# Mix projection of a two-layer encoder trunk: six of eight output tiles as block products

## What is computed

```python
mix = (jax.nn.sigmoid(gate_a) * y_a + jax.nn.sigmoid(gate_b) * y_b) @ w_out
x = x + rmsnorm(mix, g_post_mix)
```

## Time and profile before

| what | value |
|---|---|
| runs before | 1815.65, 1816.67, 1817.83 us (median 1816.67) |
| the profiled execution | 1816.42 us, its span 1814.6 us |
| PE busy | 1800.7 us, 99% of the span |
| DVE, ACT, POOL busy | 1115.6, 713.4, 1115.1 us |
| chain that ended last | PE 89%, DVE 7%, ACT 1%, issue 1% |
| granted clock of TensorE | 1.0 in the whole span |
| mix projection, layer 0 | 404.4 to 452.56 us, layer 1 the same 900 us later |

### The profile page before, as it was taken

How to read it: one execution, slowest core, us unless ns; L and a number is a source line. 1 busy time by engine, 2 the same in 40 slices (tenths; PEclk the granted TensorE clock), 3 DMA queues, 4 the chain that set the end, 5 groups by cost and what they waited for, 6 DMA issues and landing times.

```text
span 1814.6 us, 34638 instructions
## 1 busy us (share of the span) xinstructions
PE 1800.7 (99%) x14006; PEld 1742.6 (96%) x14006; DVE 1115.6 (61%) x1952; ACT 713.4 (39%) x1485; POOL 1115.1 (61%) x1292
## 2 busy tenths in 40 slices
PE   9999999999999999999999999999999999999999
PEld 8998989999999999999999988899999999999999
DVE  6676775332778568554657767752337795785554
ACT  4444453112556245332334444531135552552321
POOL 8685634656555845957666864346465558459484
...
DMA packets 76239, 170.54 MB, mean 94 GB/s; under 512 B 6384, under 2 KB 34160, under 8 KB 76080
## 3 DMA queue, kind: packets, MB, share of 16 engines
...
## 4 chain that ended last, share of the span: by engine, by line
PE 89%; DVE 7%; ACT 1%; issue 1%; POOL 0%; DMA 0%; SPq 0%; DVEq 0%; ACTq 0%; POOLq 0%
PE ps L1980 61%; PE ps L2418 6%; PE ps L2033 4%; PE ps L2448 3%; PE ps L2161 3%; PE ps L2119 2%; DVE xT L1723 1%; PE ps L2072 1%; DVE mix L1719 1%; DVE R L1364 1%; DVE xn L1364 1%; PE ps L2215 1%; DVE RF L1817 1%; PE ps L2221 1%; PE ps L2020 1%
## 5 line engine op out<-in xcount | busy, mean ns | idle before, releaser
L1980 PE MATMUL ps<-xn,wsp 128*128 128x272 f32 x7728 | 989.8, 289 | 2.1 <-ACT R L1065 0.8
L1980 PEld LDWEIGHTS ps<-xn,wsp 128*128 128x128 f32 x7728 | 974.0, 189 | 6.8 <-issue 3.0
L774 POOL TENSOR_TENSOR wsp<-raw,wsp 128x256 fp32r<-128x256 f32 x448 | 358.2, 821 | 17.9
L769 POOL CAST wsp<-raw 128x512 fp32r<-128x512 f32 x224 | 150.6, 672 | 184.6 <-DMA raw<-in_wstream 129.3
L760 POOL TENSOR_TENSOR wsp<-raw,wsp 128x256 fp32r<-128x256 f32 x208 | 151.3, 761 | 178.7 <-ACT wsp L950 178.7
L787 POOL TENSOR_TENSOR wsp<-raw,wsp 128x256 fp32r<-128x256 f32 (+1 forms) x174 | 213.3, 1248 | 6.6
L1980 PE MATMUL ps<-R,wsp 128*128 128x272 f32 x1632 | 209.1, 289 | 0.1
L1980 PEld LDWEIGHTS ps<-R,wsp 128*128 128x128 f32 x1632 | 206.0, 189 | 1.3 <-DVE xT L1393 0.5
L780 POOL CAST wsp<-raw 128x1024 fp32r<-128x1024 f32 (+2 forms) x102 | 91.3, 906 | 171.6 <-DMA raw<-in_wstream 152.7
L1364 DVE SCALAR_TENSOR_TENSOR R<-ps,R 128x512 fp32r<-128x512 f32 (+13 forms) x272 | 129.5, 499 | 65.3 <-ACT R L869 19.0
L754 POOL TENSOR_TENSOR wsp<-raw,wsp 128x512 fp32r<-128x512 f32 x64 | 94.6, 1498 | 47.3 <-DVE raw L1817 23.8
...
## 6 DMA issues: line engine op xcount, KB each, us to landing
raw<-in_wstream SPq DMA_DIRECT2D x233, 512.0 KB, 3.6
...
raw<-in_kc SPq DMA_DIRECT2D x8, 512.0 KB, 3.5
raw<-in_vc SPq DMA_DIRECT2D x8, 512.0 KB, 4.5
...
```

What stands on the lines that cost most here:

```text
L769: nc.gpsimd.tensor_copy(dst[:, 0, f], part[:, f]).then_inc(S["w_hi"], 1)
L774: ins = nc.gpsimd.tensor_tensor(dst[:, 1, f], part[:, f], dst[:, 0, f].bitcast(F32), ALU.subtract)
L1980: mm = pe.matmul(z[:, h], w[:, x, (k0 + k) * P:(k0 + k + 1) * P], rhs[:, y, k, h * HT:(h + 1) * HT], start=(k == 0 and (x, y) == (0, 0)), ...
```

## The change

`out` 0 and `out` 7 stay plain tiles. The other six become the pairs (1, 4), (2, 5), (3, 6), each made by seven block products. P1 of the first pair is put before the last k-tile of `out` 0. The activation blocks come from new work in `gated_b`: the mix tiles j = 0 to 3 and j = 4 to 7 are the two halves of k; T1, T2, T3 are sums of their column halves. `ga` 7 and `gb` 7 move ahead of `ya` 4, because the second half of the mix and its T3 are put in the place of `xn`, so that `ya` 4 to `yb` 7 follow one another without a gate tile between. ACT takes the highs of 16 more chunks per layer. x comes back in eight DMAs with chunk loads between them. The products of the mix projection use the PSUM banks in an order of their own. The helpers of the block products are now shared by both projections (their bodies are the same but for the lookup of the pair) and not shown.

```diff
+OUT = -1
+BLOCK_PAIRS = {OUT: [(1, 4), (2, 5), (3, 6)], **{i: [(j, j + NP) for j in range(NP)] for i in range(LAST)}}
...
-         ("ga", 6), ("gb", 6), ("ya", 4), ("yb", 4), ("ga", 7), ("gb", 7), ("ya", 5), ("yb", 5), ("ya", 6), ("yb", 6),
+         ("ga", 6), ("gb", 6), ("ga", 7), ("gb", 7), ("ya", 4), ("yb", 4), ("ya", 5), ("yb", 5), ("ya", 6), ("yb", 6),
...
-STREAM += [("out", j) for j in range(KT)] + [("pp", 0)] + FFN
+OUT_ORDER = [0] + [m for pair in BLOCK_PAIRS[OUT] for m in pair] + [KT - 1]
+STREAM += [("out", j) for j in OUT_ORDER] + [("pp", 0)] + FFN
...
-CAST = [c for n, c in enumerate(STREAM) if c[0] in UP and STREAM[n - 6][0] in UP]
+CAST = STREAM[ST_AT[("proj", 2)]:ST_AT[("out", 0)] + 1] + [("out", KT - 1), ("pp", 0), ("upg", 0)]
+CAST += [c for n, c in enumerate(STREAM) if c[0] in UP and STREAM[n - 6][0] in UP]
...
+                ring = [4, 5] + freed[2:] + freed[:1] + [6, 7] + freed[1:2] if t == OUT else freed + [4, 5, 6, 7]
                 continue
...
+                    sp_.wait_ge(S["mi_raw"], M_RAW[KT - 1, "B"])
                     if layer > 0:
                         sp_.wait_ge(pre["x_st"], 16)
-                    sp_.dma_start(xT[:], x_dram if layer > 0 else x_in.rearrange("(k p) t -> p k t", p=P)).then_inc(pre["x_back"], 16)
+                    x_from = x_dram if layer > 0 else x_in.rearrange("(k p) t -> p k t", p=P)
+                    behind = {1: ("out", 3), 2: ("out", 6), 3: ("out", 7), 5: ("pp", 0)}
+                    for k in range(KT):
+                        if k in behind:
+                            load_to(ST_AT[behind[k]])
+                        sp_.dma_start(xT[:, k], x_from[:, k]).then_inc(pre["x_back"], 16)
...
+                    def mix_high(j):
+
+                        kk = j % NP
+                        act.wait_ge(S["mi_raw"], M_RAW[j, "B"])
+                        ac(mix_plain(j, 0), m_raw[:, j // NP, kk], ACT.Copy).then_inc(S["mi_hi"], 1)
+                        n = G_T1 if j < NP else G_T2
+                        act.wait_ge(S["mi_raw"], M_RAW[j, n])
+                        ac(mix_part(kk, 0, n), m_keep[:, kk], ACT.Copy).then_inc(S["mi_hi"], 1)
+                        if j >= NP:
+                            act.wait_ge(S["mi_raw"], M_RAW[j, G_T3])
+                            ac(xn[:, 0, 2 * kk + 1], m_raw[:, 0, kk], ACT.Copy).then_inc(S["mi_hi"], 1)
+
...
                     for n, j in MIXES:
                         if n == "yb":
-                            act.wait_ge(S["mi_raw"], j + 1)
-                            ac(mixin[:, 0, j], tmp[0], ACT.Copy).then_inc(S["mi_hi"], 1)
+                            if j == KT - 1:
+                                plain_high(OUT, 0)
+                                for m in ("S1", "S2", "S3"):
+                                    sum_high(OUT, 0, m)
+                            mix_high(j)
                         elif n in ("ga", "gb"):
                             gate((n, j))
+                        if (n, j) in SPLIT_AFTER:
+                            cast(SPLIT_AFTER[(n, j)])
 
 
                     nc.scalar.preload_act_table_set("natural_log_exp_and_others")
-                    for j in range(KT):
-                        if j < KT - 1:
-                            z = tile(("out", j))
-                            if j == 0:
-                                act.wait_ge(S["dve_read"], dread(("yb", KT - 1)))
-                            square(0, j, z)
+                    hand_on(OUT, 0, "P1", "P2")
+                    sum_high(OUT, 0, "S4")
+                    z = tile(("out", 0))
...
+                        more = j < len(BLOCK_PAIRS[OUT]) - 1
+                        if j > 0:
+                            hand_on(OUT, j, "P1", "P2")
+                        if more:
+                            plain_high(OUT, j + 1, ("A11",))
+                        hand_on(OUT, j, "P6", "P3")
+                        if more:
+                            plain_high(OUT, j + 1, ("A22",))
+                            for m in ("S1", "S2", "S3"):
+                                sum_high(OUT, j + 1, m)
                         else:
-                            z = ptile(("out", j))
-                            for h, part in enumerate((("half", 0), ("out", j))):
-                                act.wait_ge(S["p_done"], AT[part] + 1)
-                                square_half(0, h, z[:, h])
...
-                        if j in (4, 5):
+                            cast(("pp", 0))
+                        hand_on(OUT, j, "P7", "P4")
+                        if more:
+                            sum_high(OUT, j + 1, "S4")
+                        else:
                             act.wait_ge(pre["p_in"], 16 * (layer + 1))
-                            ac(p_s[:, 0, j - 4], mix[:, j - 4, 0:T], ACT.Copy).then_inc(S["p_hi"], 1)
+                            for m in range(2):
+                                ac(p_s[:, 0, m], mix[:, m, 0:T], ACT.Copy).then_inc(S["p_hi"], 1)
+                        for m, n, t in ((1, "P3", a), (2, "P4", b)):
+                            act.wait_ge(S["dve_read"], dread((n, OUT, j)))
+                            square(0, 2 * j + m, fT[:, t])
+                        if j == 1:
+                            cast(("out", KT - 1))
+                    cast(("upg", 0))
+                    z = ptile(("out", KT - 1))
+                    for h, part in enumerate((("half", 0), ("out", KT - 1))):
+                        act.wait_ge(S["p_done"], AT[part] + 1)
+                        square_half(0, h, z[:, h])
+                    ac(halves(fT[:, KT - 1]), z, ACT.Copy).then_inc(S["act_read"], 1)
                     rsqrt_halves(0)
                     ple_tile(0)
...
-                        if j > 0:
-                            dve.wait_ge(S["mi_lo"], j)
-                        v.tensor_tensor(tmp[0], tmp[1], gate_at(("ga", j)), ALU.add).then_inc(S["mi_raw"], 1)
-                        dve.wait_ge(S["mi_hi"], j + 1)
-                        lo(mixin[:, 1, j], tmp[0], mixin[:, 0, j], "mi_lo")
+                        kk, x = j % NP, m_raw[:, j // NP, j % NP]
+                        v.tensor_tensor(x, tmp[1], gate_at(("ga", j)), ALU.add).then_inc(S["mi_raw"], 1)
+                        dve.wait_ge(S["mi_raw"], M_RAW[j, "B"])
+                        sub = v.scalar_tensor_tensor
+                        if j < NP:
+                            sub(m_keep[:, kk], x[:, HT:T], 1.0, x[:, 0:HT], ALU.mult, ALU.subtract).then_inc(S["mi_raw"], 1)
+                        else:
+                            sub(m_keep[:, kk], x[:, HT:T], 1.0, m_keep[:, kk], ALU.mult, ALU.subtract).then_inc(S["mi_raw"], 1)
+                        dve.wait_ge(S["mi_hi"], M_LO[j, "B"])
+                        lo(mix_plain(j, 1), x, mix_plain(j, 0), "mi_lo")
+                        if j >= NP:
+                            dve.wait_ge(S["mi_raw"], M_RAW[j, G_T2])
+                            y = m_raw[:, 0, kk]
+                            sub(y[:, 0:HT], x[:, 0:HT], 1.0, m_keep[:, kk], ALU.mult, ALU.subtract)
+                            sub(y[:, HT:T], x[:, HT:T], 1.0, y[:, HT:T], ALU.mult, ALU.subtract).then_inc(S["mi_raw"], 1)
+                        if j == KT - 1:
+                            weight_sum(OUT, 0, "S4")
+                        n = G_T1 if j < NP else G_T2
+                        dve.wait_ge(S["mi_hi"], M_LO[j, n])
+                        lo(mix_part(kk, 1, n), m_keep[:, kk], mix_part(kk, 0, n), "mi_lo")
+                        if j >= NP:
...
                         if n == "ya":
                             gated_a(j)
+                            if j == KT - 1:
+                                for m in ("S1", "S2", "S3"):
+                                    weight_sum(OUT, 0, m)
                         elif n == "yb":
                             gated_b(j)
...
-                        if j in (5, 6):
-                            dve.wait_ge(S["p_hi"], j - 4)
-                            lo(p_s[:, 1, j - 5], mix[:, j - 5, 0:T], p_s[:, 0, j - 5], "p_lo")
...
+                        more = j < len(BLOCK_PAIRS[OUT]) - 1
+                        collect(OUT, "P5", j, ((b, 1), (a, 1)), True)
+                        if more:
+                            for n in ("S1", "S2", "S3"):
+                                weight_sum(OUT, j + 1, n)
+                        dve.wait_ge(S["dve_read"], dread(("P5", OUT, j)))
+                        collect(OUT, "P2", j, ((a, 0),), True)
+                        if j > 0:
+                            add_squares(0, 2 * j - 1)
+                            add_squares(0, 2 * j)
+                        collect(OUT, "P7", j, ((b, 1),), False)
+                        collect(OUT, "P3", j, ((a, 1),), False)
+                        if more:
+                            weight_sum(OUT, j + 1, "S4")
+                        collect(OUT, "P4", j, ((b, 0),), True)
+                        if more:
+                            last_low(OUT, j + 1)
```

(18 more changed lines are left out.)

283 lines of the change are left out of this document (166 added, 117 removed).

## The result

The changed kernel takes 1822.05 us (median of 7, 1820.60 to 1824.52), the kernel before 1816.67: ratio 1.0032, 95% interval 1.0022 to 1.0042. By the medians it is slower by 5.4 us. The profiled execution took 1821.67 us with a span of 1819.8, 5.2 us more than before.

A forecast was written before the change was run, and what follows sets the result against it. PE, busy for 99% of the span, was taken to bound the kernel. Per layer -4.5 + 1.4 + 1.6 + 2.6 + 0.1 = +1.2 us, +2.4 in two layers: 1816.4 + 2.4 = 1818.8 us, range 1811 to 1824.5.

The forecast's parts named there:

- Saving: Three pairs of out tiles: 36 fewer matmuls per layer at 0.1253 us, 4.51 us per layer, 9.0 us in two.
- Gates tail: yb 4 to yb 7: DVE's fuller queue and locks make ya 7 and `out` 0 late, 1.4 us per layer.
- the casts cost nothing: The 16 casts of 1.04 us each lie where ACT is idle and were costed at nothing.
- Pair 0: PE waits before P4 of pair 0 for DVE's locked queue, then ACT's copy P7 to P4: 1.6 us per layer.
- pair 2: PE waits before P6 of pair 2: a chain of 13.1 us against 10.5 us of products, 2.6 us per layer.
- Pair 1 catches up: PE's wait in pair 0 lets pair 1 catch up; costed at nothing.
- Residual: POOL still at `upv` 0 when the residual begins: one or two locks, 0 to 0.6 us, taken as 0.1.
- Sum: Per layer -4.5 + 1.4 + 1.6 + 2.6 + 0.1 = +1.2 us; in two layers +2.4, total 1818.8 us.
- The likeliest case: Whole kernel: no measurable change, a time between the border lines 1813.0 and 1820.3 us; chance 0.55.
- rival 3: Slower: DVE's queue never catches up from yb 4 to P4 of pair 0, further locks reach PE: 1822.4 us; 25%.
- Rival 1: Full saving: the locks fall beside the chains, as in the second down stage: 1808 us; 8%.
- Rival 2: Half the saving: late copies to P4 and P2 are caught up, waits of 2.5 us per layer: 1812.4 us; 14%.

The follow-up runs named there:

- casts_pool: Changed kernel with ScalarE's casts of proj 2 to 7, gate chunks between and out 0 undone (13 casts), POOL making these highs again: 1827.38 us.
- p4_early: Changed kernel with only ScalarE's order altered: bank copy P7 to P4 behind the high of S1 of the next pair, not of S3: 1819.97 us.
- hand_early: Changed kernel with only ScalarE's order altered: next pair's bank copy P1 to P2 ahead of S4's high, two squares and the cast of out 7: 1818.69 us.
- cast_late: Changed kernel with only ScalarE's order altered: cast of out 7 behind pair 2's bank copy P6 to P3, not ahead of P1 to P2: 1818.94 us.
- no_lows: Changed kernel with the lows of the out pairs' weights left out, POOL writing zeros over the same places instead: 1811.51 us.
- clock_fill: Changed kernel with 18 useless matmuls more on TensorE behind P5 of pair 2, where it otherwise stands idle: 1820.41 us.
- after: The changed kernel itself, against the kernel before the change: 1822.05 us, ratio 1.0032.

## Why the prediction was right or wrong

- **Saving, -4.51 us per layer:** right.
- **Gates tail, +1.4:** measured 1.27, at `ya` 7 and the first `out` matmul. Right. But "the casts cost nothing" was too little said: casts_pool shows, in one layer, that the tail leans on the small pieces that they bring, which I did not see.
- **Pair 0, +1.6 and pair 2, +2.6:** 1.65 and 2.59, in both layers, at the products named, with two of DVE's sums in pair 1 locked (1.55 and 1.60 us) and ScalarE's copy last. p4_early, hand_early and cast_late change ScalarE's order alone and shorten or remove the gaps, no_lows takes away the locks. Right, though I had written that the trace would name ScalarE's copy: it names POOL's low and "issue".
- **"Pair 1 catches up", 0:** right, no gap.
- **Residual, +0.1:** 0.39 and 0.47. The mechanism is the one named, POOL at `upv` 0 when the residual begins: POOL's low started at 457.91, DVE's first product at 458.76 took 1.17 us instead of the 0.79 of the earlier trace rows. I had bounded it by 0 to 0.6 and taken a value near the wrong end.
- **What the sum lacked:** the clock. The step that failed is the one that cost a wait of 2.6 us at 2.6 us. In layer 0 of the profiled execution it cost 4.2, and by the medians of clock_fill and after the two waits cost 1.6 us more than their length. The forecast had no term for what the matmuls behind a wait do. Nor did it say that POOL gets time from a wait: without the wait at P6 the residual is 0.5 to 0.8 us longer (hand_early, cast_late), so a wait's length is also not what its removal gives back.
- **Sum:** +1.2 per layer became +1.5 in layer 1, where the clock held, and +3.0 in layer 0. 1818.8, with 1.6 of clock, 0.7 of residual above my 0.2, 0.7 from outside the stage, and 0.2 less by the waits, is 1821.6; the profiled execution took 1821.67.

The likeliest case, no measurable change, did not come. The time is that of rival 3, 1822.4, but not by its mechanism: no further lock stood in front of a sum, the chains were as long as I made them, and of its terms only the 0.5 us in the residual came (0.39 and 0.47). That its number is met so closely is luck. Rival 1 was no fantasy: without the lows, and so without the lock, the kernel takes 1811.5, 3.5 us above its 1808, most of it the gates tail that this rival had ignored. Rival 2's catching up did not occur.
